# A router with logits per tile, and eight small changes of order, in a two-block transformer kernel

## Chip, cores and metric

The kernel runs as one program on one core of a Trainium2 chip. The metric is the device time of one execution in microseconds, the median of several runs.

## What is computed

`x` is one sequence of 1024 rows of 1024 values, all in 32-bit floats. The first block mixes it (a gated convolution, a pooling mixer and a differential attention, joined by `mix @ w_out`), and then adds a mixture of experts. The second block has two layers; each has a latent attention, a gated linear attention, an output product and a gated projection of a second input `p`.

```python
x = x + mix @ w_out[l]
hf = rms_norm(x, ffn_norm_g[l])
x = x + hier_moe(hf, router_g_w[l], router_g_b[l], router_e_w[l], router_e_b[l], w_gate[l], w_up[l], w_down[l])
# hier_moe: 4 group logits choose one group, 4 of 16 expert logits choose two experts in it
y = y + (silu(t @ w_gate[e]) * (t @ w_up[e]) * gates[:, e:e + 1]) @ w_down[e]
# second block, layers i = 0, 1
u = rmsnorm(h, ln_mix[i]) @ w_in[i]
y_mla = mla_branch(...) * silu(gate_a)
y_gla = gla_branch(...) * silu(gate_g)
h = h + concatenate([y_mla, y_gla]) @ w_out[i]
gate = sigmoid(rmsnorm(h, ple_norm[i]) @ w_ple_gate[i])
h = h + gate * (p[i] @ w_ple_proj[i])
```

## The kernel before, in words

Rows lie in 8 tiles of 128 (`NT`), the width in 8 steps of 128 (`KD`). Each engine has its own instruction list, written out by hand, and the engines meet only at semaphores (`wait_ge`, `then_inc`). There is no planner: the order in the code is the order on the engine. Loads and stores go by SP's queue, some stores by ACT's, and gathers and scatters by POOL's.

**Split products.** Most large products are split in a rounded high part and a low rest: three single-pass matmuls a step (`accumulate_split`, L106 to L108) on operands that ACT rounds and DVE or POOL subtracts. Plain 32-bit products (`accumulate`, L96) take two instructions a step.

**Output products of the first block** (TensorE, L1796 on). 16 products `u` (two column halves of 8 tiles), alternating between banks 0 and 1; DVE adds each into `H` (L2323). In the second half ACT squares tile `t` and scales it to `xn` (`nt_act`, L503, L509), TensorE turns it (`nt_pe`, L534), DVE multiplies the gain in (`nt_dve`, L541) and SP stores `xn` and `H` to memory (L841, L842).

**Router.** The weights of 20 logits lie in `WF[:, 0]`, padded with zeros to 128 columns. They are the stationary side; `HT` streams past in two halves; ACT copies the transposed logits `lgT` (L1289), TensorE turns them back (L1817), and DVE decides (L2331 to L2379) with two exponentials by ACT. TensorE's place products (L1827 to L1829) count the rows per expert, DVE makes the tables (L2383 to L2409), a table product (L1836) orders them, and DVE raises `m_tab` (L2418). Then POOL copies the first tile's row numbers and issues the gather (L1054, L1058).

**Projection round.** `p @ w_ple_proj` of one layer runs in between: two groups of turns (`proj_turn`), 16 pieces (`proj_piece`, two matmul steps each), alternating between banks 4 and 5, evacuated by ACT (L669) and stored (L674). Two pieces stand ahead of the place products, five ahead of the table product and nine behind it; the experts begin when all have been evacuated.

**Rope.** DVE computes the angles behind the tables (L2424 to L2433), ACT takes the sine (L1300), DVE applies the sign (L2435). Only then does DVE take the first gathered rows (L2445).

**Experts.** 31 tiles (`MTILES`), each with 3 MB of weights in two buffers: gate and up (L1860, plain, and L1865 to L1867, split), the down product one tile later. SP loads the next-but-one tile's `w_gate` and `w_up` when gate-up is done (L855), POOL gathers three tiles ahead.

**Layers.** In each of the two layers 8 fills (the up projections of attention's first head) alternate between banks 0 and 1 and wait for the bank to be evacuated; DVE evacuates in order (L2671, and the rotation, L2635 to L2680). At attention's end POOL subtracts the low part of tiles 0 and 1 in one instruction of 1536 columns (L1151) and one of 512. Then come 16 output products; the weights' low part of the second column half is split by DVE one piece a tile (L2690). The turns of tiles 6 and 7 stand ahead of and behind the first gate product.

Of the kernel before, what the change touches and what calls it, by code (L numbers as in the profile page):

```python
# [6 lines left out]
F32 = mybir.dt.float32  # L7
# [104 lines left out]
def program(nc, A, out):  # L112
    ctx = ExitStack()
    with ctx:
# [147 lines left out]
        lgT = X[:, 0:1024]  # L262
# [95 lines left out]
        p_tok = [a.rearrange("p (t c) -> p t c", t=NT) for a in (slot(MXf, 0, 2), slot(HTf, 0, 2))]  # L358
        wpp = [a.rearrange("p (c n) -> p c n", c=2) for a in (slot(MXf, 2, 2), slot(WTf, 4, 2))]
        pT = [a.rearrange("p (c t) -> p c t", c=2) for a in (slot(WFf, 1, 2), slot(WTf, 6, 2))]  # L360
# [76 lines left out]
        def m_at_tile(semaphore, i, o, per=1, c=0):  # L437
# [3 lines left out]
        rw_zero, rw_in, rt_ready, rt_cp, rt_tp = (  # L441
            sem(n) for n in ("rw_zero", "rw_in", "rt_ready", "rt_cp", "rt_tp"))
# [14 lines left out]
        h_st, fh_ready = sems("h_st", 2), sem("fh_ready")  # L457
# [184 lines left out]
        def proj_turn(pe, r, c):  # L642
            if c == 0:
                pe.wait_ge(p_in, 32 * r + 16)
            if c == 1 and r == 0:
# [11 lines left out]
        def proj_piece(pe, r, i):  # L657
# [4 lines left out]
            if i >= 2:  # L662
                pe.wait_ge(pg_sg, r * 2 * NT + i - 1)
            accumulate(pe, bank(proj_banks[r] + i % 2), [(pT[r][:, c, t * P:(t + 1) * P], wpp[r][:, c, n * HALF:(n + 1) * HALF]) for c in range(2)]).then_inc(pg_ready, 1)

        def proj_evac(act, r, i):
            t, n = i // 2, i % 2
            act.wait_ge(pg_ready, r * 2 * NT + i + 1)
            act.activation(proj[r][t][:, n * HALF:(n + 1) * HALF], bank(proj_banks[r] + i % 2), ACT.Copy).then_inc(pg_sg, 1)  # L669
# [105 lines left out]
        def _(sp):  # L775
# [60 lines left out]
            sp.wait_ge(rw_zero, 1)  # L836
            sp.dma_start(WF[:, 0, :, 0:4], A["router_g_w"][0].rearrange("(k p) c -> p k c", p=P)).then_inc(rw_in, 16)
            sp.dma_start(WF[:, 0, :, 4:20], A["router_e_w"][0].rearrange("(k p) c -> p k c", p=P)).then_inc(rw_in, 16)
            for t in range(NT):
                sp.wait_ge(n_xn, NT + t + 1)  # L840
                sp.dma_start(xn_dram[t * P:(t + 1) * P, :], xn[:, t % 2, :]).then_inc(xn_st[t % 2], 16)  # L841
                sp.dma_start(h_dram[t * P:(t + 1) * P, :], H[:, t, :]).then_inc(h_st[2 * t // NT], 16)  # L842
            sp.wait_ge(wo_ready, 2 * NT)
            rows_load(sp, 0)
            matrix_load(sp, 0)
# [21 lines left out]
            for o in range(2):  # L867
                load_gu(0, o)
                if o == 0:
                    sp.wait_ge(p_tp, 2)  # L870
                else:
                    sp.wait_ge(pg_ready, 2 * NT)
                load_d(0, o)
# [1911 lines left out]
```

## Time and profile before

| | us |
|---|---|
| median of 3 runs | 2340.37 |
| lowest, highest | 2336.68, 2347.42 |
| profiled execution | 2345.37 |
| its span | 2343.6 |
| TensorE busy | 2242.4 (96%) |
| VectorE busy | 1361.3 (58%) |
| ScalarE busy | 1073.9 (46%) |
| GpSimd busy | 516.9 (22%) |

The span is the time between the first and the last instruction of the profiled execution. Busy time of TensorE is modelled, since its matmuls overlap; two starts tell more than one duration.

### The profile page before, as it was taken

How to read it: one execution, taken by the hardware profiler on the slowest of the kernel's cores; microseconds unless marked ns; L12 is line 12 of the kernel's file. 1: busy time of each engine (PE TensorE's matmuls, PEld its weight loads, DVE VectorE, ACT ScalarE, POOL GpSimd, SP SyncE). 2: the span in 40 equal slices, each digit the busy share in tenths (PEclk: the TensorE clock that was granted, in tenths of full speed). 3: DMA queues.
4: the chain of work that ended last, by engine and by line, in shares of the span. 5: the costliest groups of instructions: out<-in, count | busy, mean ns of one | idle time of the engine just before them, and what ended most of it. 6: DMA issues, size and time to landing. Idle time of an engine off the chain costs nothing.

```text
span 2343.6 us, 30001 instructions
## 1 busy us (share of the span) xinstructions
PE 2242.4 (96%) x11196; PEld 1769.2 (75%) x11196; DVE 1361.3 (58%) x2095; ACT 1073.9 (46%) x1723; POOL 516.9 (22%) x512
## 2 busy tenths in 40 slices
PE   7999888989999999999999999999999999999998
PEld 6877566845666666888878888787788877888886
DVE  5884585255666754666337775445477327776354
ACT  4222775225555656555334443435555343445242
POOL 2157243112233334211220011102212220002001
PEclk9999999999999999999999999999999999999999
DMA  5210210258999965111110013122111110013112
GB/s 130 86 37 1 74 71 11 102 203 322 356 367 348 339 227 169 37 37 37 48 30 23 1 37 144 46 81 75 45 37 37 34 49 16 12 37 144 37 54 99
DMA packets 146490, 236.40 MB, mean 101 GB/s; under 512 B 44096, under 2 KB 100672, under 8 KB 134464
## 3 DMA queue, kind: packets, MB, share of 16 engines
q1 hardware_dynamic: 135136, 209.53, 25.5%
q0 software_dynamic: 8928, 16.80, 3.0%
q10 hardware_dynamic: 2304, 8.39, 0.9%
q8 instruction: 82, 1.34, 0.2%
q14 instruction: 40, 0.33, 0.0%
HBM read 208.98 MB, written 41.42 MB: 107 GB/s over the span
## 4 chain that ended last, share of the span: by engine, by line
PE 73%; DMA 7%; DVE 5%; ACT 3%; issue 2%; POOL 1%; SPq 1%; POOLq 0%; DVEq 0%; ACTq 0%
PE ps L106 13%; PE ps L108 13%; PE ps L107 13%; PE ps L96 7%; DMA h_dram<-X 7%; PE ps L2113 2%; PE ps L1860 2%; PE ps L1753 1%; PE ps L2066 1%; PE ps L2065 1%; PE ps L2067 1%; PE ps L1735 1%; PE ps L1733 1%; PE ps L1734 1%; PE ps L2104 1%
## 5 line engine op out<-in xcount | busy, mean ns | idle before, releaser
L108 PE MATMUL ps<-HT_hi,WF_lo 128*128 128x512 f32 x800 | 313.1, 391 | 0.0
L106 PE MATMUL ps<-HT_hi,WU_hi 128*128 128x512 f32 x704 | 283.2, 402 | 7.8 <-DVE H_lo L2492 2.6
L107 PE MATMUL ps<-H_lo,WU_hi 128*128 128x512 f32 x704 | 274.7, 390 | 0.0
L107 PE MATMUL ps<-WT_lo,HT_hi 128*128 128x512 f32 x656 | 256.3, 391 | 0.0
L1090 POOL TENSOR_TENSOR WF_lo<-WF,WU_hi 128x1024 fp32r<-128x1024 f32 x42 | 114.5, 2727 | 435.7 <-ACT WU_hi L1371 435.7
L106 PE MATMUL ps<-W_hi,HT_hi 128*128 128x512 f32 x472 | 186.8, 396 | 2.9 <-DVE WT_lo L2690 2.9
L108 PE MATMUL ps<-W_hi,MIX_lo 128*128 128x512 f32 x480 | 188.0, 392 | 0.0
L108 PEld LDWEIGHTS ps<-HT_hi,WF_lo 128*128 128x128 f32 x800 | 150.7, 188 | 32.3
L106 PEld LDWEIGHTS ps<-HT_hi,WU_hi 128*128 128x128 f32 x704 | 132.6, 188 | 41.6 <-issue 3.8
L107 PEld LDWEIGHTS ps<-H_lo,WU_hi 128*128 128x128 f32 x704 | 132.7, 189 | 29.3 <-issue 2.9
L107 PEld LDWEIGHTS ps<-WT_lo,HT_hi 128*128 128x128 f32 x656 | 123.9, 189 | 25.2 <-issue 0.5
L1860 PE MATMUL ps<-WT,MIX 128*128 128x512 f32 x248 | 114.8, 606 | 6.7 <-DVE MIX L2445 5.1
L527 POOL TENSOR_SCALAR ss<-ss 128x1 f32<-128x1 f32 x56 | 20.5, 365 | 444.6 <-ACT ps L503 245.5
L503 ACT ACTIVATE ps<-H 128x1024 f32<-128x1024 f32 x32 | 32.9, 1028 | 182.0 <-DVE H L2730 112.4
L106 PEld LDWEIGHTS ps<-W_hi,HT_hi 128*128 128x128 f32 x472 | 89.5, 190 | 21.8 <-DVE WT_lo L2690 3.7
L108 PEld LDWEIGHTS ps<-W_hi,MIX_lo 128*128 128x128 f32 x480 | 90.6, 189 | 19.2
L2704 DVE TENSOR_REDUCE sm<-ps 128x1 f32<-128x1024 f32 x64 | 78.4, 1225 | 44.6 <-PE ps L2104 44.1
L2463 DVE TENSOR_TENSOR MIX_lo<-MIX,WK_hi 128x1024 fp32r<-128x1024 f32 x62 | 73.2, 1222 | 50.9 <-ACT WK_hi L1316 50.9
L1860 PEld LDWEIGHTS ps<-WT,MIX 128*128 128x128 f32 x248 | 47.4, 194 | 56.9 <-issue 46.2
L2452 DVE TENSOR_TENSOR WT_lo<-WT,WK_hi 128x1024 fp32r<-128x1024 f32 x62 | 73.0, 1219 | 19.8 <-ACT WK_hi L1306 16.1
L1604 ACT ACTIVATE xn<-ps,sm 128x1024 f32<-128x1024 f32 x64 | 71.6, 1119 | 25.6 <-DVE sm L2705 25.6
L1306 ACT ACTIVATE WK_hi<-WT 128x1024 fp32r<-128x1024 f32 x62 | 62.1, 1050 | 34.7 <-DMA WT<-in_w_up 34.7
(486 smaller groups left out, 5581.8 us busy)
## 6 DMA issues: line engine op xcount, KB each, us to landing
WT<-in_w_gate SPq DMA_DIRECT2D x31, 1024.0 KB
WT<-in_w_up SPq DMA_DIRECT2D x31, 1024.0 KB
MIX<-in_w_down SPq DMA_DIRECT2D x31, 1024.0 KB
WF<-in_w_in SPq DMA_DIRECT2D x48, 512.0 KB, 3.8
WT<-in_w_out SPq DMA_DIRECT2D x6, 2048.0 KB, 8.7
H<-h_dram SPq DMA_DIRECT2D x24, 512.0 KB, 11.4
H<-in_x SPq DMA_DIRECT2D x16, 512.0 KB, 7.3
h_dram<-H SPq DMA_DIRECT2D x16, 512.0 KB, 3.6
```

Of the source, the lines that this page charges most:

```text
L96: mm = pe.matmul(o, l, r, start=(i == 0), stop=(i == last))
L106: pe.matmul(o, lh, rh, start=(i == 0), stop=False)
L107: pe.matmul(o, lh, rl, start=False, stop=False)
L108: mm = pe.matmul(o, ll, rh, start=False, stop=(i == last))
L1090: pool.tensor_tensor(WFr[:, w, :, 0:n], WF[:, w, :, 0:n], wu_hi[:, w, :, 0:n].bitcast(F32), ALU.subtract).then_inc(ul_ready, 1)
L1306: act.activation(wgu_hi[:, g, :, :], wgu[:, p, g, K0:KD, :], ACT.Copy).then_inc(m_gh, 1)
L1604: act.activation(xn[:, g % 2, :], psf[:, (2 + 2 * (g % 2)) * HALF:(4 + 2 * (g % 2)) * HALF], ACT.Exp, scale=MLA_SCALE, bias=sm[:, g % 2, 1 ...
L1860: pe.matmul(to, hgT[:, p, k, :], wgu[:, p, :, k, :], start=(k == 0), stop=False)
L2113: tp = pe.transpose(bank(6 + half, P, k * P), xn[:, q % 2, (4 * half + k) * P:(4 * half + k + 1) * P], ident[:, :])
L2452: ins = dve.tensor_tensor(wgu_lo[:, p, g, K0:KD, :], wgu[:, p, g, K0:KD, :], wgu_hi[:, g, :, :].bitcast(F32), ALU.subtract)
L2463: ins = dve.tensor_tensor(wd_lo[:, p, k, :], wd[:, p, k, :], down_hi_at(i, o)[:, k, :].bitcast(F32), ALU.subtract)
L2704: hc.link(dve.tensor_reduce(sm[:, g % 2, 0:1], psf[:, (2 + 2 * (g % 2)) * HALF:(4 + 2 * (g % 2)) * HALF], AX.X, ALU.max))
```

## The change

The edits, in the order of the program:

- **Router logits per tile.** The stationary side is now the 128 x 128 piece of `HT`, the moving side 20 columns of `WF`; the logits of all tiles lie in bank 6 with the rows in partitions, so that `lgT`, its copies, its turns and the padding go. ACT's squares go to `rope` in place of banks 6 and 7. The turn of tile `t - 2` and the logits of tile `t - 3` stand inside output product `u`, between steps 4 and 5; DVE multiplies the gain in before its add.
- **Projection round.** `p` is loaded during the products, into `H`'s first tiles in place of `MIX`; three banks; 6 pieces ahead of the place products, 6 ahead of the table product, 3 behind, the last one behind the first turn of gathered rows. ACT splits the first expert's weights before the last pieces.
- **Rope** goes between the adds of four output products, ACT's sine behind tile 5.
- **First gather** takes the row numbers from the table itself. SP loads the second expert's weights only when the gather has landed.
- **Layers.** The first 8 fills take banks 0 to 7 and don't wait. POOL's 1536 columns go in three instructions. DVE splits the weights two pieces a tile in tiles 2 to 5. The turn of tile 6 stands inside the first gate product.

```diff
-        turn_banks = [[(4, 5), (4, 5)], [(0, 1), (3, 5)]]
-        proj_banks = (4, 0)
+        turn_banks = [[(0, 1), (0, 1)], [(0, 1), (3, 5)]]
+        proj_banks = ((5, 4, 3), (0, 1))
...
+        def fill_at(f):
+            return FILLS[f][2] if f < 8 else fill_bank(f)
...
+                if t == 4:
+                    sp.wait_ge(h_st[0], 64)
+                    rows_load(sp, 0)
+                if t == 5:
+                    matrix_load(sp, 0)
             sp.wait_ge(wo_ready, 2 * NT)
-            rows_load(sp, 0)
-            matrix_load(sp, 0)
             sp.wait_ge(experts_set, 1)
...
+            load_gu(0, 0)
+            load_d(0, 0)
+            sp.wait_ge(m_hg[0], 16)
+            load_gu(0, 1)
+            sp.wait_ge(pg_ready, 2 * NT)
+            load_d(0, 1)
...
+                if isinstance(i, int) and o == 0:
+                    pool.sem_inc(m_tok, 1)
+                    pool.indirect_dma_start(out=hg[:, p, :], ..., in_offset=IndirectOffsetOnAxis(ap=tabs[:, 0:1, 0:1], axis=0), ...)
+                    return
...
-                pool.tensor_tensor(MIXr[:, 0:6, 0:2 * P], MIX[:, 0:6, 0:2 * P], HTr[:, 0:6, 0:2 * P].bitcast(F32), ALU.subtract).then_inc(r0_lo, 1)
+                for k in range(0, 6, 2):
+                    pool.tensor_tensor(MIXr[:, k:k + 2, 0:2 * P], MIX[:, k:k + 2, 0:2 * P], HTr[:, k:k + 2, 0:2 * P].bitcast(F32), ALU.subtract).then_inc(r0_lo, 1)
...
+                nt_act(act, 1, t, lambda t: (wo_evac, NT + t + 1), stored=xn_st, squares=rope)
+                if t == 5:
+                    act.wait_ge(rope_set, 1)
+                    act.activation(ang, ang, ACT.Sin).then_inc(rope_set, 1)
+                    act.preload_act_table_set(LOG_EXP)
...
-            act.wait_ge(pg_ready, 2 * NT)
-            gate_up_hi(0, 0)
+            for t in range(1, NT):
+                proj_out(act, 0, t)
+                if t == NT - 2:
+                    gate_up_hi(0, 0)
+            proj_store(act, 0, NT - 1)
...
+            def logits(t):
+                if t == 0:
+                    pe.wait_ge(rw_in, 64)
+                pe.wait_ge(n_ht, ht_ready(1, t + 1))
+                mm = accumulate(pe, bank(6, 20, 20 * t), [(HT[:, k, t * P:(t + 1) * P], WF[:, 0, k, 0:20]) for k in range(KD)])
+                if t == NT - 1:
+                    mm.then_inc(rt_ready, 1)
...
-                    out_product(u, range(KD))
+                    out_product(u, range(0, 5))
                     if u >= NT + 2:
                         nt_pe(pe, 1, t - 2)
+                    if u >= NT + 3:
+                        logits(t - 3)
+                    out_product(u, range(5, KD))
+            logits(NT - 3)
+            proj_turn(pe, 0, 0)
+            for t in (NT - 2, NT - 1):
+                nt_pe(pe, 1, t)
+            for t in (NT - 2, NT - 1):
+                logits(t)
+            proj_turn(pe, 0, 1)
+            for i in range(6):
                 proj_piece(pe, 0, i)
...
-            for i in range(2, 7):
+            for i in range(6, 12):
...
-            for i in range(7, 2 * NT):
+            for i in range(12, 2 * NT - 1):
                 proj_piece(pe, 0, i)
-            pe.wait_ge(pg_sg, 2 * NT)
...
             turn_rows(0, 0)
+            proj_piece(pe, 0, 2 * NT - 1)
+            pe.wait_ge(pg_sg, 2 * NT)
             experts(pe, expert_pe)
...
-                    b = fill_bank(f)
+                    b = fill_at(f)
-                    if part != 1:
+                    if part != 1 and f >= 8:
                         pe.wait_ge(f_evac[b], fill_evac(L, f) - 1)
...
-                nt_pe(pe, L * 2 + 3, NT - 2)
...
+                        accumulate_split(..., (lambda k: nt_pe(pe, L * 2 + 3, NT - 2) if k == 4 else None) if u == 0 else None).then_inc(pg_ready, 1)
...
+                if NT <= u < NT + 4:
+                    angles(u - NT)
...
-                        weights_lo(1, t)
+                        if 2 <= t < 6:
+                            weights_lo(1, 2 * (t - 2))
+                            weights_lo(1, 2 * (t - 2) + 1)
```

The diff's parts are, in order, the declarations, SP, POOL, ACT, TensorE and DVE. `angles(part)` holds the ten instructions of L2425 to L2433 in four parts. The stores of `H` now count on three semaphores in place of two, for 4, 2 and 2 tiles.

## Rows read from the trace of the kernel before

**Rows 1.** The page's first part: engine, busy us, share, instructions.
```profile
PE 2242.4 (96%) x11196; PEld 1769.2 (75%) x11196; DVE 1361.3 (58%) x2095; ACT 1073.9 (46%) x1723; POOL 516.9 (22%) x512
```
**Rows 2.** Waits of TensorE, whole span: total us, times, longest.
```profile
PE ps L534 <- ACT xn L509: 6.4, 3, 2.1
PE ps L96 <- DVE HT_hi L2680: 5.5, 4, 1.4
...
PE ps L2113 <- DVE PTa L2717: 5.3, 2, 2.6
PE ps L106 <- DVE WT_lo L2690: 2.9, 2, 1.5
```
**Rows 3.** Timeline of TensorE, router stretch: start, us, instruction, [idle before <- releaser].
```profile
472.87 1.09 PE L534 MATMUL ps<-ident,xn 128*128 128x128 f32 x8 [2.13 <-ACT xn L509]
473.80 7.03 PE L96 MATMUL ps<-HT,WF 128*128 128x512 f32 x16
...
496.32 5.26 PE L96 MATMUL ps<-MIX,WF 128*128 128x512 f32 x8 [1.18 <-ACT WF L654]
503.10 0.40 PE L1827 MATMUL ps<-X,ones 128*128 128x16 f32 x2 [1.52 <-DVEq L2379]
...
513.46 3.78 PE L1836 MATMUL ps<-X,MIX 128*128 128x62 f32 x32 [0.38 <-DVE MIX L2409]
517.08 15.67 PE L96 MATMUL ps<-MIX,WF 128*128 128x512 f32 x36
533.44 1.16 PE L1849 MATMUL ps<-ident,MIX 128*128 128x128 f32 x8 [0.69 <-ACT HT L669]
538.33 6.43 PE L1860 MATMUL ps<-WT,MIX 128*128 128x512 f32 x8 [3.73 <-DVE MIX L2445]
```
**Rows 4.** Stages: length, busy us by engine, granted clock, DMA share, GB/s.
```profile
496.00:499.00 3.00, 2.68 (x3) 1.18 (x4) 2.28 (x12) 0.49 (x2) 0.00 (x0) 0.51 0.00 0
538.00:541.00 3.00, 2.67 (x3) 1.18 (x4) 3.00 (x4) 1.97 (x3) 0.00 (x0) 0.50 0.91 332
...
1524.00:1527.00 3.00, 3.00 (x11) 2.46 (x10) 2.24 (x2) 1.93 (x2) 0.00 (x0) 0.52 1.04 401
```
**Rows 5.** Timeline of VectorE, router stretch.
```profile
492.04 0.52 DVE L2331 TENSOR_TENSOR X<-ps,X 128x80 f32<-128x80 f32 x2 [9.01 <-PE ps L1817]
...
536.20 0.75 DVE L2435 TENSOR_SCALAR rope<-X,kc 128x1024 f32<-128x1024 f32 x1 [8.79 <-ACT X L1300]
```
**Rows 6.** Timeline of GpSimd, the first gathers, and its DMA queue in 540:541.
```profile
519.91 1.72 POOL L1058 DMA_INDIRECT MIX<-xn_dram,X  x1 [1.00 <-POOL X L1054]
...
530.01 0.18 POOL L1054 COPY X<-X 128x1 int32<-128x1 int32 x1 [5.75 <-DMA MIX<-xn_dram,X]
535.44 1.01 POOL L1058 DMA_INDIRECT MIX<-xn_dram,X  x1 [5.25 <-PE ps L1849]
...
q0 software_dynamic: 70, 0.15, 39.2%
```
**Rows 7.** Timelines of VectorE and TensorE at layer 0's output and gate products.
```profile
1513.75 0.69 DVE L2730 TENSOR_TENSOR H<-ps,H 128x512 f32<-128x512 f32 x1 [0.19 <-PE ps L108]
1520.09 0.69 DVE L2730 TENSOR_TENSOR H<-ps,H 128x512 f32<-128x512 f32 x1 [0.17 <-PE ps L108]
...
1523.05 1.59 PE L534 MATMUL ps<-ident,xn 128*128 128x128 f32 x8 [2.13 <-ACT xn L509]
1531.85 0.47 PE L106 MATMUL ps<-W_hi,HT_hi 128*128 128x512 f32 x1
```
**Rows 8.** Timeline of SP's queue, first and last weight request on release; one stage.
```profile
547.71 0.35 SPq L855 DMA_DIRECT2D WT<-in_w_gate  x1
...
842.59 0.34 SPq L855 DMA_DIRECT2D WT<-in_w_gate  x1
...
600.00:760.00 160.00, 152.65 (x608) 103.63 (x607) 106.45 (x131) 90.40 (x119) 47.74 (x56) 1.00 1.01 359
```
**Rows 9.** Timelines of TensorE and VectorE, layer 0's first fills and scores.
```profile
1220.20 1.98 PE L96 MATMUL ps<-X,WF 128*128 128x512 f32 x4 [1.33 <-DVE HT_hi L2680]
1228.89 0.47 PE L2100 MATMUL ps<-HT_hi 128*128 128x512 f32 x1
...
1223.56 0.69 DVE L2671 TENSOR_TENSOR H_lo<-ps,HT_hi 128x512 fp32r<-128x512 f32 x1
```
**Rows 10.** Timelines of GpSimd and VectorE at the end of layer 0's attention.
```profile
1413.76 3.46 POOL L1151 TENSOR_TENSOR MIX_lo<-MIX,HT_hi 128x1536 fp32r<-128x1536 f32 x1 [3.47 <-ACT MX_hi L1585]
...
1415.13 2.63 DVE L2710 TENSOR_SCALAR xn<-xn,sm 128x1024 f32<-128x1024 f32 x1
```

More of the change, by code:

```diff
@@ L260, in program @@
         cpw = xn[:, 0, 512:1024].rearrange("p (k n) -> p k n", k=2)
-        lgT = X[:, 0:1024]
         rb = X[:, 1024:1044]
@@ L929, in layer @@
                 sp.wait_ge(a_s, L * 4 * NT + 4 * NT)
-                for half in range(2):
-                    sp.wait_ge(h_st[half], L * 64 + 64)
+                for j in range(3):
+                    sp.wait_ge(h_st[j], (L + 1) * 16 * STORED[j])
                 settle(sp, settled)
@@ L1079, in _ @@
                 gather(0, o)
-            for half in range(2):
-                pool.wait_ge(h_st[half], 64)
+            for j in range(3):
+                pool.wait_ge(h_st[j], 16 * STORED[j])
             experts(pool, expert_pool)
@@ L2309, in _, with angles @@
                     mix1_lo(dve, g - (NB - 1))
+            C1 = 6.28125
+            C2 = float(np.float32(np.round((2 * np.pi - C1) * 2.0 ** 20) * 2.0 ** -20))
+            C3 = float(2 * np.pi - C1 - C2)
+            MAGIC = 1.5 * 2.0 ** 23
+            def angles(part):
+                if part == 0:
+                    dve.wait_ge(row_in, 16)
+                    chain.link(dve.tensor_copy(ang, pos_i))
+                    chain.link(dve.tensor_scalar(ang, ang, kc[:, K_INV:K_INV + 1], None, ALU.mult))
+                    chain.link(dve.tensor_scalar(turns, ang, 1.0 / (2 * np.pi), kc[:, K_OFF:K_OFF + 1], ALU.mult, ALU.add))
+                if part == 1:
+                    chain.link(dve.tensor_scalar(turns, turns, MAGIC, None, ALU.add))
+                    chain.link(dve.tensor_scalar(turns, turns, -MAGIC, None, ALU.add))
+                if part in (2, 3):
+                    for c in ((C1, C2), (C3,))[part - 2]:
+                        chain.link(dve.scalar_tensor_tensor(out=ang, in0=turns, scalar=-c, in1=ang, op0=ALU.mult, op1=ALU.add))
+                if part == 3:
+                    chain.link(dve.tensor_scalar(ang, ang, kc[:, K_RAD:K_RAD + 1], 3.1415925, ALU.add, ALU.min))
+                    dve.tensor_scalar(ang, ang, -3.1415925, None, ALU.max).then_inc(rope_set, 1)
             for t in range(2, 4):
@@ L2323, in _ @@
                 dve.tensor_tensor(hh, bank(u % 2), hh, ALU.add).then_inc(wo_evac, 1)
[L2324 to L2325 removed]
+                if NT <= u < NT + 4:
+                    angles(u - NT)
             for t in (NT - 2, NT - 1):
                 nt_dve(dve, 1, t, vec1[:, V_FG:V_FG + 8])
[L2328 removed]
+            dve.wait_ge(rope_set, 2)
+            dve.wait_ge(n_ss, 2 * NT)
+            dve.tensor_scalar(rope[:, :], ang, kc[:, K_SIGN:K_SIGN + 1], None, ALU.mult).then_inc(rope_set, 1)
+            dve.wait_ge(rope_set, 3)
+            dve.wait_ge(rt_ready, 1)
             dve.wait_ge(rw_in, 64)
[L2330 to L2331 removed]
+            chain.link(dve.tensor_tensor(lg, bank(6, 160).rearrange("p (t e) -> p t e", t=NT), rb.unsqueeze(1).to_broadcast([P, NT, 20]), ALU.add))
             dve.wait_ge(iotas, 3)
```

111 lines of the change are left out of this document (34 added, 77 removed).

## The prediction

> **What bounds the kernel now.** I read the page's first part, then TensorE's waits, then the timelines of the places the diff touches. TensorE is busy for 96% of the span [rows 1], so an edit pays only where it takes away TensorE work, a TensorE wait, or half-speed clock. The waits that the diff touches are small and countable [rows 2]: scaled rows (`xn`) 6.4 us in three waits, the turned head queries (`HT_hi`) 5.5 us in four, split weights 2.9 us in two, attention's transposes behind DVE 5.3 us in two. Of the three in the first row one is the router's (2.13 us) [rows 3] and two are the layers'. The router stretch is the one large hole: from the end of the last output product (about 470.7) to the first expert matmul at 538.33 are 67.6 us, in which TensorE waits 2.13, 1.18, 1.52, 0.38 and 3.73 us [rows 3] and runs twice at the 1.2 GHz level of its clock [rows 4].
>
> **Router: TensorE's work.** Old logits: two groups of 16 instructions, 7.0 us each, 14.0 us, then 8 transposes of about 1.1. New: 8 tiles x 8 steps x 2 instructions = 128, each with new weights and only 20 columns. No row has 20 columns; the nearest is the table product, 62 columns, 32 instructions in 3.78 us, 0.118 us each [rows 3]. Ends: 0.055 (the loads half as dear) and 0.19 (nothing hidden), so 7 to 24 us; I take 0.118, so 1.9 us a tile and 15.1 in all. TensorE's work does not shrink; what changes is the order.
>
> The Trainium skill (TensorE: Matmul & The Clock Gate, LDWEIGHTS) puts a load at stationary columns over 1.2 per ns, about 107 ns for 128 columns whatever streams past; by it, an estimate, the logits take 13.7 us, 1.4 less than by the 62-column row. It speaks against turning the operands round (128 columns loaded for 20 used), and the two figures agree that nothing is gained in work.
>
> **Router: the order, step by step.** A product step is 6.34 us (the two DVE adds 1513.75 and 1520.09 in rows 7 have the same 24 matmuls and one turn; 0.87 us of turn leaves 0.228 a matmul). Five logits groups go inside the products: the end moves from 470.7 to about 480.2. Then: logits 5 to 482.0; first `p` turn to 483.0; turn of tile 6 to 484.0 (its `xn` comes 2.9 us after the last add starts, which the logits and the `p` turn now hide; before, it was the 2.13 wait); turn of tile 7 to 485.3; logits 6 and 7 to 489.2. DVE gets them 2.8 us earlier than 492.04 [rows 5]. Its decision takes 11.0 us (492.04 to the place products at 503.10), so ready at 500.3. Meanwhile TensorE does the second `p` turn, waits 1.2 for its copy, and does six projection pieces of 4 x 0.43 = 1.72 us (0.43 from the 36 instructions in 15.67), to 501.6. Place products to 503.1, which is 1.4 earlier. DVE's tables take 9.0 more (504.5 to 513.46): 512.1, under pieces 6 to 11, which end at 513.4. The table product then sits where it sat (513.46), but 12 pieces are behind it and not 7. So `m_tab` is at 518 as before, and what counts afterwards is the first gather.
>
> Before, the gather was issued at 519.91 after a copy and landed about 530.0 (the third gather's copy waits for it) [rows 6]: the second expert's 2 MB were ahead of it and beside it. Now there is no copy (1.5 us earlier: issue 518.4) and those 2 MB wait for the gather. The third gather, issued 535.44 to 536.45, is still being served in 540:541 [rows 6]: 4.6 us behind the end of its issue. With a first issue of 1.72 us that gives a landing at 524.7; ends 523 and 530 (nothing gained from the queue). The Trainium skill (DMA: Bandwidth & Descriptors, the GpSimd path) has about 2.0 us plus bytes over 436 GB/s, 3.2 us for 0.5 MB, so by it, an estimate, the landing is 523.3 and the forecast 1.4 us lower.
>
> TensorE has done pieces 12 to 14 by 522.4, waits 2.4, turns the gathered rows (1.1), does piece 15 over DVE's 1.3 us, and waits for its copy: gate-up of tile 0 starts at 528.3, **10.0 us** before 538.33. The rope arithmetic that held DVE until 536.20 [rows 5] lies in the four product steps of tiles 0 to 3, where DVE has 4 us idle of each 6.3; ACT's sine and two table loads (3.6 us) fit the 8.2 us step of tile 5. Clock: gate-up's 8 instructions took 6.43 us for 3.44 [rows 3, 4], behind a 3.7 us gap. The new gap of 2.4 may do it again, half as long; I count **+2.0** of the 3.0. Against it, the two 1.5 MB loads (`p` rows, mix gain) now directly precede tile 2's weights: 4 us of queue where rows before had 3 of slack; **-1.0**. Router: 11.0, ends 4 and 14.
>
> Does it survive the expert phase, whose DMA runs at a share of 1.01 from 600 to 760 [rows 8]? A tile's load is asked for when its buffer frees; an earlier start moves the requests too. The period between first releases, 547.71 and 842.59 [rows 8], is 294.9 / 28 = 10.53 us. Only a backlog at the start is not moved, the 1.0 above.
>
> **Layers, twice each.** (a) The first 8 fills take banks 0 to 7 and wait for nothing. The waits of 1.33 and 1.40 go, with some 0.3 of restart: **3.0**. The next reader, the first scores, needs fill 5 evacuated; DVE's serial chain has fill 4's evacuation at 1223.56 and the next 0.7 later, 1225.0, before the 1225.7 at which TensorE now arrives instead of 1228.89 [rows 9]. The fourth wait in that row, 0.8, stays. (b) The POOL subtraction of 1536 columns took 3.46 us, and a DVE scaling under it 2.63 us for 0.75 [rows 10]; TensorE waited 2.63 [rows 2]. In three parts of 1.15, DVE gets in after the second: **1.0**, ends 0 and 1.9. The Trainium skill (SBUF — State Buffer, the shared port pair) says the pair is an exclusive lock for a whole instruction, which is what 2.63 for 0.75 shows; by it the gain is 1417.2 - 16.2 = 1.0 if DVE wins the next turn, and 0 if POOL does. (c) Weight halves of the second column half are split in tiles 2 to 5, not one a tile up to the last: the wait of 1.45 [rows 2] goes and DVE has 3 us idle in each of those steps: **1.45**. (d) Turn of tile 6 moves into the first gate product. Before: turn of tile 5, wait 2.13, tile 6's turn at half clock (1.59), product 0 partly at half clock (0.52 in 1524:1527 [rows 4]), turn 7, product 1 at 1531.85 [rows 7]. After: the product can start behind turn 5 at 1520.9, since the last add ends at 1520.78; 24 x 0.228 + 2 x 0.87 gives 1528.2: **3.65**, ends 2 and 3.7. The sigmoid table and tile 7's chain end 1 us before product 2 asks. Per layer 9.1; twice, **18.2**.
>
> **Sum.** The profiled execution took 2345.37, 1.77 outside its span of 2343.6. 2345.4 - 11.0 - 18.2 = 2316.2. It stands 5.0 above the median of the runs, 2340.37; 2340.4 - 29.2 = 2311.2. I say **2311**.
>
> **Rivals.** *R1, the gather's landing does not gain* (0.15): DMA engines are slow with 4 KB rows whatever else runs. For: 4.6 us already with one queue nearly idle. Against: 8.4 before under 2 MB. Landing 530 leaves the router 5, all 23: 2317. *R2, the expert phase eats the router's gain* (0.12): the 2 MB and 3 MB pushed from idle into full DMA time put tiles 1 to 4 behind. For: share 1.01. Against: requests move along. Router 0, all 18: 2322. *R3, only half the layers' waits go* (0.15): (a) and (d) hand the wait to DVE or ACT one step on. Layers 9, all 20: 2320. *R4, slower* (0.04): the expert phase becomes DMA-bound throughout, because gathers, scatters and weights meet differently. It decides from a mean period of 10.53 + 29.2/28 = 11.57 us; at 11.7 it costs 32.8 and gives 2344. Against: from 600 to 760 TensorE was busy for 152.65 of 160 us even so. *R5, no change* (0.04): short router matmuls drop TensorE's clock during the products; seven steps of 6.3 at half speed in part, 1.7 us each, 12 us, with R3: 2332.
>
> **Chances.** Forecast 0.50, R1 to R5 0.50. I widen the likeliest case (2305 to 2317) to R2 and R3 and leave out R4 and R5: 2302 to 2325. Faster or slower counts from 0.5%, 11.7 us, about what a measurement of this kernel can tell. Faster takes the forecast, R1 to R3 nearly whole: 0.89. Same: R5 and part of R2, 0.07. Slower 0.04, part of R4 and what I have not seen.
>
> **What would show it.** The first expert matmul at 527 to 530; the table product still near 513 with 12 pieces ahead; logits near 1.9 us a tile; the first gather landing 6 us behind its issue; no waits by `HT_hi` but one a layer; no wait by `xn` at the gate; POOL's three parts of 1.15 and a DVE scaling under 1.9; expert period 10.5. I am wrong if the table product comes later than 515, if the period rises above 10.9, or if the first scores wait for DVE.

## The result, and the profile after

The changed kernel takes 2329.07 us (median of 11 runs, 2325.93 to 2333.74). The kernel before, run beside it, takes 2344.49 us (11 runs, 2336.68 to 2348.84). The ratio is 0.9934, 95% interval [0.9921, 0.9946], so the change gains 15.4 us. The forecast was 2311, and 2329.07 lies above its range. The three runs that stood in the time before (median 2340.37) were on the low side; the profiled 2345.37 was close to what eleven runs gave. That is 4 of the 18 us. The other 14 are the router.

The profiled execution took 2330.26 us, its span is 2328.5. The page's first part answers to [rows 1]. TensorE is busy for 96% of the span as before:

```profile
PE 2239.7 (96%) x11284; PEld 1777.7 (76%) x11284; DVE 1359.2 (58%) x2094; ACT 1074.4 (46%) x1722; POOL 517.9 (22%) x514
```

TensorE's waits over the whole span (total us, times, longest) answer to [rows 2]. The waits for `xn` at L534, for `HT_hi` at the fills (L96) and for `WT_lo` have left the list, and attention's went from 5.3 to 3.4. Two are new in size: 7.0 us once at a gate-up product, and 1.2 us twice for the first sigmoid (`WF`).

```profile
PE ps L1879 <- issue: 7.0, 1, 7.0
...
PE ps L2134 <- DVE PTa L2747: 3.4, 2, 1.7
PE ps L106 <- ACT WF L1662: 2.4, 2, 1.2
```

**The router stretch.** TensorE's timeline answers to [rows 3]. The logits take 1.86 us a tile, as forecast (1.71 from one start to the next instruction's, 481.71 to 483.42). But the last two tiles take 4.60 us for 3.7, the second turn of `p` 1.95 for 1.07, and the six pieces 13.22 us, where 24 instructions of 0.43 are 10.3. The place product comes at 507.97 (forecast 501.6), the table product at 519.40 (forecast 513.4), the first gate-up at 535.45 (forecast 528.3, before 538.33), the third tile's only at 561.42.

```profile
481.71 1.86 PE L96 MATMUL ps<-WF,HT 128*128 128x20 f32 x16
...
487.36 4.60 PE L96 MATMUL ps<-WF,HT 128*128 128x20 f32 x32 [0.22 <-DVE HT L546]
491.79 1.95 PE L655 MATMUL ps<-ident,H 128*128 128x128 f32 x8
494.91 13.22 PE L96 MATMUL ps<-H,MIX 128*128 128x512 f32 x24 [1.17 <-ACT MIX L661]
507.97 0.29 PE L1847 MATMUL ps<-X,ones 128*128 128x16 f32 x2
...
519.40 3.68 PE L1856 MATMUL ps<-X,MIX 128*128 128x62 f32 x32
...
530.19 1.37 PE L1868 MATMUL ps<-ident,MIX 128*128 128x128 f32 x8 [1.90 <-DMA MIX<-xn_dram,X]
...
535.45 3.70 PE L1879 MATMUL ps<-WT,MIX 128*128 128x512 f32 x8 [0.69 <-ACT HT L677]
...
561.42 5.51 PE L1879 MATMUL ps<-WT,MIX 128*128 128x512 f32 x8 [6.96 <-issue]
```

The stages (length, TensorE's busy us, granted clock, DMA share, GB/s) answer to [rows 4]. A clock of 0.5 is the 1.2 GHz level. It holds from 490 to past 498, and again around 530 and 560.

```profile
490.00:494.00 4.00, 3.74 (x18) 0.51 0.21 83
494.00:498.00 4.00, 3.09 (x4) 0.50 0.00 0
498.00:502.00 4.00, 4.00 (x8) 0.71 0.00 0
530.00:534.00 4.00, 3.81 (x12) 0.63 0.71 224
558.00:562.00 4.00, 0.58 (x1) 0.54 1.04 430
```

VectorE's rows answer to [rows 5]. It gets the logits at 492.05, when it got them before (492.04), waits 2.19 us for an exponential that stands behind the turn's copies on ACT, and then 4.06 us for the late place products:

```profile
492.05 0.33 DVE L2379 TENSOR_TENSOR X<-ps,X 128x160 f32<-128x160 f32 x1 [2.89 <-issue]
495.01 0.18 DVE L2401 TENSOR_REDUCE X<-X 128x8 f32<-128x32 f32 x1 [2.19 <-ACT X L1309]
509.30 0.17 DVE L2431 TENSOR_SCALAR X<-ps 128x16 int32<-128x16 f32 x1 [4.06 <-PE ps L1849]
```

GpSimd's rows answer to [rows 6]. The gather is issued at 525.11 and has landed by 530.30, 5.2 us later, where the forecast had 6.3:

```profile
525.11 1.31 POOL L1064 DMA_INDIRECT MIX<-xn_dram,X  x1 [38.55 <-issue]
...
530.30 0.18 POOL L1068 COPY X<-X 128x1 int32<-128x1 int32 x1 [1.78 <-DMA MIX<-xn_dram,X]
```

**Why the third tile waits 6.96 us.** SP's queue answers to the first of [rows 8]. SP takes its list in order. Behind `w_down` of the second expert it waits for the projection's stores to land, issues the next layer's rows and the gain, and only then asks for the third tile's weights, at 548.73. That wait is 11.1 us long (5.5 before, when the third tile's request came behind it at 547.71, on release, and TensorE did not wait for the weights):

```profile
SPq L641 <- DMA proj_dram<-HT: 11.1, 1, 11.1
```

In the kernel with both remedies (below: these loads last, logits of 64 columns) the request comes 6.65 us behind the start of the first gate-up, at 533.73 for 527.08; 535.45 + 6.65 is 542.1, so here it is 6.6 us late.

```profile
535.51 0.34 SPq L870 DMA_DIRECT2D MIX<-in_w_down  x1
546.93 0.40 SPq L641 DMA_DIRECT2D HT<-in_p  x1
...
548.73 0.35 SPq L865 DMA_DIRECT2D WT<-in_w_gate  x1
```

The stores are late beside 3 MB of weights, which the change has put just ahead of them. The view of DMA issues in 530 to 550 gives, for the last two stores, the median from issue to landing. Of the changed kernel:

```profile
proj_dram<-HT ACTq DMA_DIRECT2D x2, 512.0 KB, 10.5
```

and of the kernel before:

```profile
proj_dram<-HT ACTq DMA_DIRECT2D x2, 512.0 KB, 4.4
```

The Trainium skill (DMA: Bandwidth & Descriptors, Queues, rings and completion order) has each DMA engine take turns between the queues it has work for, one packet at a time; 10.5 us beside SP's weights against 4.4 agrees. In the kernel with the loads behind tile 4's request the stores are as slow (9.1 us) and hold nothing up at the third tile, because SP no longer waits for them there.

**The layers.** TensorE's timeline, layer 0, answers to the later lines of [rows 2, 7, 9]. The first row is that of the first layer's input products that waits for `H_lo` ("layer row" from here on); before it stands at 912.88. Before and after, the stages start at 912.88 / 915.82, 1246.93 / 1246.60, 1418.51 / 1417.24, 1621.04 / 1616.23 and (layer 1) 1930.60 / 1923.26. So up to the layers the change costs 2.9 us, and over the layers it gains 18.0: 10.3 to the second layer's start and 7.8 behind it. The experts' period is 10.56 us (570.12 to 844.60, 26 tiles) and was 10.53, so rival R4 plays no part.

```profile
915.82 0.50 PE L106 MATMUL ps<-HT_hi,WU_hi 128*128 128x512 f32 x1 [0.99 <-DVE H_lo L722]
...
1246.60 0.50 PE L106 MATMUL ps<-CQ_hi,UQb_hi 128*128 128x512 f32 x1 [0.80 <-DVE HT_hi L2710]
1417.24 1.16 PE L2134 MATMUL ps<-ident,xn 128*128 128x128 f32 x8 [1.70 <-DVE PTa L2747]
...
1532.47 0.50 PE L106 MATMUL ps<-W_hi,HT_hi 128*128 128x512 f32 x1 [1.18 <-ACT WF L1662]
1616.23 0.47 PE L106 MATMUL ps<-HT_hi,WU_hi 128*128 128x512 f32 x1 [0.68 <-issue]
...
1923.26 0.47 PE L106 MATMUL ps<-CQ_hi,UQa_hi 128*128 128x512 f32 x1 [0.73 <-issue]
```

At attention's end GpSimd's three parts and VectorE's scaling answer to [rows 10]: the scaling takes 1.70 us for 2.63.

```profile
1413.42 4.20 POOL L1166 TENSOR_TENSOR MIX_lo<-MIX,HT_hi 128x512 fp32r<-128x512 f32 x3 [3.48 <-ACT MX_hi L1601]
...
1414.79 1.70 DVE L2740 TENSOR_SCALAR xn<-xn,sm 128x1024 f32<-128x1024 f32 x1
```

### The profile page after: what moved, and what is told of

Same layout as the page of the kernel before. It is cut to its first block, busy times and chain, and to the rows that moved or that the text cites. A ratio compares the mean times of both kernels' runs of the same rounds, so it can differ in the third digit from the quotient of the medians.

```text
span 2328.5 us, 30180 instructions
## 1 busy us (share of the span) xinstructions
PE 2239.7 (96%) x11284; PEld 1777.7 (76%) x11284; DVE 1359.2 (58%) x2094; ACT 1074.4 (46%) x1722; POOL 517.9 (22%) x514
## 4 chain that ended last, share of the span: by engine, by line
PE 74%; DMA 7%; DVE 4%; ACT 3%; issue 3%; POOL 1%; SPq 1%; POOLq 0%; DVEq 0%; ACTq 0%
PE ps L106 13%; PE ps L108 13%; PE ps L107 13%; PE ps L96 8%; DMA h_dram<-X 7%; PE ps L1879 2%; PE ps L2134 2%; PE ps L1769 1%; PE ps L1749 1%; PE ps L1751 1%; PE ps L1750 1%; PE ps L2087 1%; PE ps L2086 1%; PE ps L2088 1%; PE ps L2125 1%
## 5 line engine op out<-in xcount | busy, mean ns | idle before, releaser
L2218 DVE SCALAR_TENSOR_TENSOR H<-H,vec 128x1024 f32<-128x1024 f32 x60 | 76.9, 1282 | 1.5
```

The costliest lines, as they stand in the source:

```text
L2218: o = dve.scalar_tensor_tensor(out=y_cv[:, c, :], in0=uu, scalar=w, in1=y_cv[:, c, :], op0=ALU.mult, op1=ALU.add)
```

## The experiments

My theory after the result: the layers gain what was forecast; the router's gain is there, and two things take it back one behind the other, the half clock at the logits and SP's wait ahead of the third tile's weights. The rival: the expert phase eats any router gain, whatever the cause of its lateness (R2 as the prediction put it). Each ratio is to the kernel before, run beside it on the same chip. "Under the changed kernel" compares medians from different chips, between which the kernel before moved by up to 3.7 us (2342.12 to 2345.80); where such a difference is small, the ratios with their intervals decide.

### The two halves of the change

The layers' edits alone on the kernel before. 

> The kernel before with the layers' edits alone (fills in banks 0 to 7, the subtraction in three, weight halves two a tile, the turn of tile 6 inside the first gate product). Theory A, the layers gave all and the router nothing or less: 18 us faster than before, 2326, and about 3 us faster than the whole change. Theory B, the two traces' comparison misleads and both parts gave some 8 us: 2336.

Measured: 2330.25 us, ratio 0.9941 [0.9925, 0.9958], 14.6 us faster. Its trace has TensorE in the first layer at 913.08 (before 912.88) and at the second layer's start at 1921.35 (before 1930.60); with the end that is 17.2 us in the profiled execution. By the ratio the gain is 13.8 us, 9.8 to 17.6: theory A's sign and size, but below its 18.

The router's edits alone. 

> The whole change without the layers' edits. Theory A: 0 to 4 us slower than before (2344 to 2348), with TensorE's wait of about 7 us before tile 2's gate-up and about 10 us at half clock during logits and projection. Theory B: 8 us faster, 2336.

Measured: 2345.21 us, ratio 1.0004 [0.9992, 1.0017]: nothing. So of theories A and B it is A. Yet its first gate-up starts at 526.32, 12 us before that of the kernel before (3.7 of them lie in the opening: its first output product starts at 374.06, in the kernel before at 377.72). The rows show how it is given back: the second tile's weights come 2.22 us late, the third's 6.74, and beside those waits the products run at half clock (5.37 us for 3.70).

```profile
526.32 3.70 PE L1873 MATMUL ps<-WT,MIX 128*128 128x512 f32 x8 [0.69 <-ACT HT L672]
535.89 5.37 PE L1873 MATMUL ps<-WT,MIX 128*128 128x512 f32 x8 [2.22 <-DMA WT<-in_w_up]
554.62 6.46 PE L1873 MATMUL ps<-WT,MIX 128*128 128x512 f32 x8 [6.74 <-issue]
```

### SP's wait, and the width of the logits

```diff
-            sp.wait_ge(out_st, 16 * NT)
-            rows_load(sp, 1)
-            sp.wait_ge(rope_set, 3)
-            sp.dma_start(mix_gain, ...)
-            experts(sp, expert_sp)
+            def expert_sp_then(i, o):
+                expert_sp(i, o)
+                if isinstance(i, int) and o == 2:
+                    sp.wait_ge(out_st, 16 * NT)
+                    rows_load(sp, 1)
+                    sp.wait_ge(rope_set, 3)
+                    sp.dma_start(mix_gain, ...)
+            experts(sp, expert_sp_then)
```

> The whole change, but SP's wait for the projection stores, and the 1.5 MB loads behind it (p rows of the second round, mix gain), stand behind the requests for the weights of tile 4. Theory A, SP's order: the request for tile 2's weights goes out at about 542 and not 548.7, the wait of 7.0 us before its gate-up shrinks to under 2, and the kernel is 5 to 8 us faster than the change, 2323. Theory B, DMA is full anyway: the wait only moves to tile 3 or 4 and the time stays at 2329.

Measured: 2322.83 us, ratio 0.9912 [0.9894, 0.9929], 6.2 us under the changed kernel. The wait at the third tile is gone. That is theory A. But the 1.5 MB now lie ahead of another tile's weights, where TensorE waits 5.31 us at 586.54, though the stores have landed long before: the bytes cost something too, and a part of the loss has moved, not left. From the first gate-up to the layer row it takes 376.2 us, against 380.4 in the changed kernel and 373.9 with the loads last (table below), so 4.2 of 6.4 us have left.

```diff
-                mm = accumulate(pe, bank(6, 20, 20 * t), [(HT[:, k, ...], WF[:, 0, k, 0:20]) for k in range(KD)])
+                mm = accumulate(pe, bank(6, 64, 64 * t), [(HT[:, k, ...], WF[:, 0, k, 0:64]) for k in range(KD)])
```

> The whole change, but each logits matmul streams 64 columns and not 20 (the 44 more are never read). Same instructions, same loads; by the table product's 62 columns at 0.118 us each the work costs the same. Theory A, the 10 us at half clock come from long stretches in which the array streams little: the half-clock stretch gets shorter, the place products come 2 to 5 us earlier than 508, the kernel is 1 to 4 us faster than the change. Theory B, the idle moments of 0.4, 0.2 and 1.2 us bring it: nothing changes, 2329.

Measured: 2323.11 us, ratio 0.9913 [0.9897, 0.9929], 6.0 us under the changed kernel (4.9 by the ratios, whose intervals just touch). Forty-four more columns cost nothing that shows: two tiles take 3.79 us, and 3.65 with 20 columns at the same clock (below). That is theory A of the expectation, with a larger gain than its 1 to 4 us. The six pieces take 10.57 us, not 13.22, and the first gate-up starts at 527.54; the forecast had 528.3. The loss at the third tile is all there (7.45).

```profile
485.31 3.79 PE L96 MATMUL ps<-WF,HT 128*128 128x64 f32 x32 [0.22 <-DVE HT L546]
...
491.15 10.57 PE L96 MATMUL ps<-H,MIX 128*128 128x512 f32 x24 [1.18 <-ACT MIX L661]
501.55 0.29 PE L1847 MATMUL ps<-X,ones 128*128 128x16 f32 x2
...
527.54 3.70 PE L1879 MATMUL ps<-WT,MIX 128*128 128x512 f32 x8 [0.69 <-ACT HT L677]
...
554.07 5.51 PE L1879 MATMUL ps<-WT,MIX 128*128 128x512 f32 x8 [7.45 <-issue]
```

Its stages (columns as above) show the clock at its 2.4 GHz level in the router stretch:

```profile
490.00:494.00 4.00, 2.85 (x7) 1.00 0.00 0
...
498.00:502.00 4.00, 4.00 (x13) 1.00 0.34 135
```

### The turn ahead of the logits, and the second expert's weights early

`proj_turn(pe, 0, 1)` stands ahead of `logits(6)` and `logits(7)`. 

> The changed kernel, but the projection's second turn stands ahead of the logits of tiles 6 and 7 instead of behind them. Theory A (what the router costs is the half clock that the 20-column logits bring, and a turn that is late by its copies): the 1.17 us in which TensorE waits for the turn's last copy before the first piece goes, the place products come 1 to 2 us earlier, and the half clock stays, so that the time is 0 to 2 us under the changed kernel's, 2327 to 2329. Theory B (it is the sum of waits of TensorE ahead of the first piece that lets the clock fall): without the wait the half-clock stretch is gone and the place products come 5 us earlier, 2322 to 2324.

Measured: 2326.84 us, ratio 0.9919 [0.9902, 0.9935]; 2.2 us under the changed kernel, 3.5 by the ratios, whose intervals overlap. By time that is theory A, by the trace theory B: with 20 columns but without the wait of 1.17 us, the clock stays at 2.4 GHz, the place products come at 501.83, and the first gate-up at 527.55.

```profile
487.96 3.65 PE L96 MATMUL ps<-WF,HT 128*128 128x20 f32 x32
491.45 10.55 PE L96 MATMUL ps<-H,MIX 128*128 128x512 f32 x24
...
527.55 3.70 PE L1879 MATMUL ps<-WT,MIX 128*128 128x512 f32 x8 [0.69 <-ACT HT L677]
537.10 5.37 PE L1879 MATMUL ps<-WT,MIX 128*128 128x512 f32 x8 [2.21 <-DMA WT<-in_w_up]
```

So eight us at the first gate-up became two to four in the time (3.4 at the layer row). The rest went into waits of 2.21 and 6.67 us and into half clock behind them (clock 0.65 from 548 to 560, 0.79 from 900 to 908). How narrow products and the wait share the fall of the clock is not settled: either remedy lifts it. That either does is not one trace's luck. All five kernels with 20 columns and the second turn behind the logits have the half clock there (the six pieces take 12.08 to 13.22 us); none of the five with 64 columns has it (10.52 to 10.57), nor this one.

`sp.wait_ge(m_hg[0], 16)` is taken out ahead of `load_gu(0, 1)`, whose buffer nothing else uses. 

> The changed kernel, but the second expert's gate and up weights (2 MB) are requested without waiting for the first gather. Theory A (the expert phase is bound by the weights' stream from its first request on, and in the 25 us before the first gather lands the DMA engines stand mostly idle): 2 MB, 5 us of full DMA, are drawn ahead; the third tile's weights come earlier, the stores of the last projection no longer lie behind 3 MB, and the time falls 2 to 5 us, to 2324 to 2327. Theory B (the gather then lands behind these 2 MB): tile 0's gate-up product comes 3 to 5 us later and the time is the changed kernel's or up to 3 us above it, 2329 to 2332.

Measured: 2330.16 us, ratio 0.9936 [0.9919, 0.9952]: the changed kernel's time, theory B. The gather, issued at 525.11 as there, lands at 535.8 and not at 530.2, and TensorE waits 7.48 us for it. In exchange the third tile's wait shrinks from 6.96 to 1.51. The change's hold on these weights is right for the gather; it is worth nothing here because another wait stood behind it. Without that other wait, in the two kernels at the end of the next section, it is worth 4.3 us from the logits of tile 5 to the layer row.

```profile
535.77 1.97 PE L1867 MATMUL ps<-ident,MIX 128*128 128x128 f32 x8 [7.48 <-DMA MIX<-xn_dram,X]
...
562.36 3.67 PE L1878 MATMUL ps<-WT,MIX 128*128 128x512 f32 x8 [1.51 <-issue]
```

### The remedies together

From here on the store wait and the loads stand behind the requests for the gate and up weights of tile 29 and the down weights of tile 28, tiles counted from 0 (`o == MTILES - 4`).

Loads last, logits of 64 columns. 

> Two remedies together: logits products of 64 columns, and the wait for the stores with the next layer's rows behind the request of tile 28's weights instead of ahead of tile 2's. Each remedy alone (the rows behind tile 4's) gave 6 us. Theory A (they lie one behind the other on the way to the layers and add up): 12 us under the changed kernel, 2317, with no wait over 1.5 us at tile 2 and no half clock at the logits. Theory B (the weights' stream bounds the expert phase, so that only one of them counts): 2322 to 2324.

Measured: 2317.29 us, ratio 0.9883 [0.9865, 0.9901], 11.8 us under the changed kernel: theory A, though a wait of 2.48 us at the second tile stays.

TensorE's timeline, with the layer's row:

```profile
527.08 3.70 PE L1882 MATMUL ps<-WT,MIX 128*128 128x512 f32 x8 [0.69 <-ACT HT L677]
536.91 3.67 PE L1882 MATMUL ps<-WT,MIX 128*128 128x512 f32 x8 [2.48 <-DMA WT<-in_w_up]
...
902.26 0.51 PE L106 MATMUL ps<-HT_hi,WU_hi 128*128 128x512 f32 x1 [0.98 <-DVE H_lo L722]
```

SP's queue asks for the third tile's weights 8 us sooner than in the kernel with wide logits alone (541.75):

```profile
533.73 0.34 SPq L865 DMA_DIRECT2D WT<-in_w_gate  x1
```

Loads last alone, 20 columns. 

> The changed kernel with the store wait and the next layer's rows behind the request of tile 28's weights; the logits keep their 20 columns. Wide logits alone gave 6 us, both remedies 12. Theory A (the remedies add up): 6 us under the changed kernel, 2323. Theory B (with the loads last rather than behind tile 4, the new wait of 5.3 us at tile 5 is gone too, so that this is worth more than 6): 2318 to 2320, and the half clock at the logits is worth little once the loads are last. Theory C (without wide logits the start is so late that the weights are there anyway): 2327 to 2329.

Measured: 2320.62 us, ratio 0.9907 [0.9885, 0.9929]. Its interval holds theories A and B. C's 2327 lies at its very edge, the slowest of six runs took 2324.54, and the third tile has no wait in the trace (its gate-up starts at 546.24), so C is out. The half clock at the logits is there (six pieces 12.26 us): this is the wait's removal alone.

The router's part with both remedies, without the layers' part. 

> The router's part of the change alone on the kernel before, with both remedies: logits products of 64 columns, and the next layer's rows behind the request of tile 28's weights. The router alone gave nothing. Theory A (the router and the expert phase hold a gain of some 12 us that the half clock and the late weights of tile 2 had taken back; it is independent of the layers): 2331 to 2335. Theory B (both remedies help only because the layers' part shifts the later stages): above 2340.

Measured: 2333.08 us, ratio 0.9955 [0.9939, 0.9972]. The same part without them was at 1.0004, and the intervals lie far apart. This is theory A and the clearest single comparison of the study.

With the second turn ahead and the second expert's weights early as well. 

> As the kernel with both remedies, and also the second turn ahead of the logits of tiles 6 and 7, and the second expert's weights requested without waiting for the gather. Theory A (the weights' stream is what bounds the expert phase once the waits at its start are gone, so requests made earlier are worth their whole DMA time): 3 to 5 us under the kernel with both remedies, 2312 to 2314. Theory B (the gather lands later behind the early weights and tile 0 starts later by as much): within 1 us of it, about 2317.

Measured: 2320.04 us, ratio 0.9897 [0.9880, 0.9914]: not faster than both remedies, so theory A is out. The gather, issued at 513.54, lands 9.7 us later (TensorE waits 6.49 for it at 523.21) and the first gate-up is at 528.33.

The same with those weights held back, as in the change. 

> The changed kernel with 64-column logits, the second turn ahead of the logits of tiles 6 and 7, and the loads last; the second expert's weights wait for the gather as in the change. Theory A (each us at the turn is a us at the first gather): 1 to 2 us under the kernel with both remedies, 2315 to 2316. Theory B (the weights' stream bounds the expert phase, so that a start a us earlier is given back by tile 8): 2317 to 2318.

Measured: 2316.16 us, ratio 0.9887 [0.9869, 0.9904]. It has the lowest median of all kernels run; from 2317.29 (ratio 0.9883) it can't be told apart, and so its theories A and B can't either.

Profiled executions differ by up to 6 us in their openings (the logits of tile 5 start between 475.48 and 481.72). Most of it is there before any edit acts: the first output product starts between 373.57 (loads last) and 378.99 (second weights early), and from 240 to 280 the granted clock is 1.00 in the first of these and 0.91 in the changed kernel. So the router is best read from the logits of tile 5 to the layer row:

| kernel | logits of tile 5 | first gate-up | layer row | us, logits to row | us, gate-up to row |
|---|---|---|---|---|---|
| kernel before | | 538.33 | 912.88 | | 374.6 |
| router's part alone | 476.02 | 526.32 | 911.40 | 435.4 | 385.1 |
| changed kernel | 481.71 | 535.45 | 915.82 | 434.1 | 380.4 |
| second weights early | 481.72 | 541.84 | 915.81 | 434.1 | 374.0 |
| turn ahead | 481.72 | 527.55 | 912.38 | 430.7 | 384.8 |
| loads behind tile 4's request | 478.61 | 532.01 | 908.17 | 429.6 | 376.2 |
| 64 columns | 479.66 | 527.54 | 908.60 | 428.9 | 381.1 |
| both, turn ahead, second weights early | 476.20 | 528.33 | 902.41 | 426.2 | 374.1 |
| loads last | 475.48 | 527.38 | 901.31 | 425.8 | 373.9 |
| router's part with both | 477.66 | 525.76 | 901.98 | 424.3 | 376.2 |
| both | 479.36 | 527.08 | 902.26 | 422.9 | 375.2 |
| both, turn ahead | 479.59 | 527.60 | 901.45 | 421.9 | 373.9 |

The last column shows what the experts' phase gives back. The four kernels with SP's wait ahead of the third tile's weights and the second weights held take 380.4 to 385.1 us, all others 373.9 to 376.2, as the kernel before. So the expert phase does not eat a router gain as such: with the wait gone the earlier start arrives at the layers.

The forecast was 480.2 for the logits and 912.88 - 11.0 = 901.9 for the layer row, so 421.7. That is what the last kernel shows. The changed kernel is 12.4 above it, and 1.5 more lie in its opening, 1.1 of them already at its first output product (378.85, in the kernel before 377.72).

### The layers' parts

The first eight fills in their own banks, alone. 

> The kernel before with one part of the layers' change: the first eight fill pieces in the banks of their own. Theory A (the 3.0 us of waits a layer behind the first attention stage go, and nothing takes their place): 6 us faster, 2339 to 2340. Theory B (the pieces go into banks that something else still holds, or the wait comes back at the next product): 0 to 3 us faster.

Measured: 2339.03 us, ratio 0.9988 [0.9976, 1.0000]; in the profiled executions, from the first layer's row to the end, 5.3 us. The two waits are gone (1246.93 less 1210.42 was 36.5, and is 33.3), and nothing waits in their place. But at 1412.09 the first layer's transposes behind the unchanged wait of 2.64 us run at half clock (1.77 us for 1.16), and the stretch from there to the edge stage is 1.4 us longer. By time the gain is 3.1 us, at the edge of theory B; by the trace it is theory A less this.

The gate product's turns and the weights' halves, alone. 

> The kernel before with two parts of the layers' change: the gate product's last turns inside its first product, and the low halves of its weights spread over units. Theory A (the forecast's 1.45 + 3.65 us a layer): 10 us faster, 2335. Theory B (what the changed kernel's trace shows: 3.5 us a layer at the gate product, and another 2.5 a layer at the edge stage behind it, which belongs to this part because TensorE no longer drops its clock there): 12 us faster, 2333. Theory C (the new wait on the first sigmoid takes the gain): 7 us faster, 2338.

Measured: 2337.35 us, ratio 0.9971 [0.9958, 0.9983]; 7.2 us from the first layer's row to the end. By time it is 4.8, less than any of the three theories. Here too the first layer's transposes fall to half clock, and the edge stage keeps its own:

```profile
1418.51 1.94 PE L2113 MATMUL ps<-ident,xn 128*128 128x128 f32 x8 [2.63 <-DVE PTa L2717]
```

This row starts at 1418.51, as in the kernel before, and all that this kernel edits in the first layer comes later. So its edits can't have brought the half clock. Over all traces, a wait of 2.63 us ahead of these transposes (six kernels with the subtraction in one instruction, two layers each) is followed by a granted clock under 0.7 over the next 4 us in 7 of 12 places, the router's part alone among them; a wait of 1.70 (ten kernels with three parts) in none of 20.

All of the layers' edits but the split of GpSimd's subtraction. 

> The kernel before with the layers' change except for the split of the GpSimd subtraction at attention's end. The fills alone gave 3.1, the gate's turn and halves alone 4.8, all of the layers' change 14.6. Theory A (the split carries what is missing: with the whole instruction TensorE waits 2.6 us instead of 1.7 and then runs at the 1.2 GHz level there and again at the edge stage, 3 us a layer): 6 to 9 us faster than before, 2336 to 2338, with a half clock near 1412 and near 1625. Theory B (the parts add up when both are in, the split itself is worth its 0.9 a layer): 12 to 13 us faster, 2332.

Measured: 2329.70 us, ratio 0.9945 [0.9926, 0.9964]. From the first layer's row to the end it gains 14.7 us, all of the layers' edits 17.2, and the two parts above added 12.5. So in these traces the split carries about 2.5 us, its own 2 and little else: theory B. By time the two kernels can't be told apart (0.9945 and 0.9941). The half clock behind the transposes is there in the first layer (0.68 over 4 us) and not in the second, so what the split is worth depends on how often it is there. The edge stage's half clock is gone in this kernel too.

The edge stage (1621.04 to 1930.60 before, 309.6 us) needs a remark, since no run was meant for it alone. It takes 307.9 us with the layers' edits alone, where VectorE still idles 2.04 us ahead of its `H_lo`, and 306.9 to 307.0 in every kernel with the router's part, also in those without any of the layers' edits, where it idles 1.03. The first of these rows is of the layers alone, the second of the router alone:

```profile
1617.94 2.36 DVE L2498 TENSOR_TENSOR H_lo<-MIX,HT_hi 128x1024 fp32r<-128x1024 f32 x2 [2.04 <-issue]
...
1624.36 2.36 DVE L2516 TENSOR_TENSOR H_lo<-MIX,HT_hi 128x1024 fp32r<-128x1024 f32 x2 [1.03 <-POOL rs L528]
```

The edit of the router's part that reaches this place is the third semaphore of `H`'s stores: VectorE's wait at tile 4 was for four stores and is now for two. No run changes it by itself, so this reading is argued from the code and these traces.

## Why the prediction was wrong

**Layers: 18.2 forecast and 18.0 found in the profiled pair, of which 15.5 by the forecast's own terms.** The mechanism of all four terms held; that the sum came out so near is in part luck, and the layers' edits alone gave 14.6 us by time, at most 17.6 by the interval. (a) 3.0 a layer: 3.3. (b) 1.0: 0.9. The Trainium skill (SBUF — State Buffer, the shared port pair) has the lock held for a whole instruction; a scaling of 1.70 us for 0.75 that begins among three parts of 1.4 each (4.20 in all) agrees, and DVE won the next turn. (c) and (d) together 5.1: 3.5 up to the edge stage. Here a size failed: TensorE waits 1.18 us for the first sigmoid at product 2, which the forecast had ready 1 us ahead. The edge stage gave about 2.5 that no term had: before, it ran at the 1.2 GHz level in part (0.79 from 1632 to 1640) and had a wait of 2.58 for `H_lo`; after, its clock stays up and the wait is 1.66. Some 0.9 of it comes with the router's part, as said above. Two errors of opposite sign.

**Router: wrong, +11.0 forecast and -2.9 found** (1.1 of the 2.9 stand before the first output product, ahead of every edit). The order of steps and the gather came out as forecast, and so did the clock behind the first gate-up: it took 6.43 us and takes 3.70, where the forecast counted +2.0. The first gate-up itself came 2.9 us earlier than before and not 10.0, and the experts' phase then gave back 5.8. The failed steps are these.

- "Logits 6 and 7 to 489.2", and all behind it, reckoned every instruction at the full clock. The order held, and so did 1.9 us a tile. But TensorE fell to 1.2 GHz at 490, in a stretch for which the forecast had no clock term. With the clock kept up, by either remedy, the forecast's landmarks come out to a us: place products at 501.55 and 501.83 (501.6), first gate-up at 527.54 and 527.55 (528.3). Some of that nearness is luck, since the openings of these two executions lie 2.1 us apart: counted from the logits of tile 5, the first gate-up comes 47.9 and 45.8 us later (forecast 48.1), in the changed kernel 53.7. Rival R5 named the mechanism (short router matmuls drop the clock) but put it inside the products, where it did not happen, and gave it 0.04.
- "The two 1.5 MB loads now directly precede tile 2's weights: -1.0." This priced 1.5 MB in a queue. What it put at nothing was the instruction ahead of them: SP's wait for the stores. It had cost nothing before, when the stores landed in 4.4 us; with 3 MB beside them it made the third tile's request 6.6 us late, and TensorE waited 6.96. Every run moved the wait and the 1.5 MB together, so their shares are not measured apart: that the wait has most of it is read from the late request, and that the bytes are not free from the 5.31 us at tile 5. R2 had the place (tiles 1 to 4 behind, router 0, layers 18) and, with 0.12, came nearest in its parts: 2322 on the forecast's basis, 2326 on that of eleven runs. But it named the bytes as the cause, and the order of SP's list went first. R5 with R3 lay nearer by number on the forecast's basis (2332), but took half of the layers' waits to stay, and they went.
- "12 pieces behind it, so what counts is the first gather": right, and its landing took 5.2 us against 6.3. The hold on the second expert's weights saves 5.6 us of landing, as the early-weights kernel shows.
- A reading: the prediction lists five waits of TensorE in the old router stretch. The timeline has four more (1.38, 0.69, 1.18 and 0.69 us, 3.9 in all). No term of the sum rests on the list.

By my own test (table product later than 515) the forecast was refuted at 519.40.

## What to carry to other kernels

When a step moves ahead of a wait in an in-order queue, ask what that wait ends on, and what the change has put beside it: a wait that had slack can become the bound without a line of its own being edited. A gain of TensorE time is safe only where the clock stays up around it; before moving small products next to a short wait, look at the granted clock of that stretch, and try wider products or another order, which here cost nothing. Where two losses lie one behind the other, removing one shows only part of what it holds (a start 8 us earlier gave 2 to 4 us), so judge a remedy with the other in place.

## What I had not expected of the hardware

- 32 instructions with 64 streamed columns take 3.79 us and with 20 columns 3.65 at the full clock; the wider ones kept TensorE at 2.4 GHz in a place where the narrow ones, followed by a 1.17 us wait, did not.
- A gather of 512 KB took 5.2 us from issue to landing when the first expert's weights had just landed and mainly a store of 512 KB ran beside it, and 10.7 us with the second expert's 2 MB still in the queues.
- The same instructions behind the same wait can run at either level of the clock from one execution, or one layer, to the next: half clock followed the 2.63 us ahead of attention's transposes in 7 of 12 places and the shorter wait of 1.70 us in none of 20. A single trace of each kernel is not enough to lay such a stretch to an edit; here one case lay ahead of the edit.
